# Forgetting attention: last value tiles in pieces between its first steps, results over done keys and queries

## What is computed

```python
k = kvf[..., :1024]; v = kvf[..., 1024:2048]          # kvf = rms_norm(x, kv_norm) @ w_kv, 16 heads of 64
log_f_cum = cumsum(log_sigmoid(kvf[..., 2048:] + b_forget))
q = h @ w_q
for blk in range(4):                                   # 128 queries, e = their last key
    s = q[:, :, s0:e] @ k[:, :, :e].T * 64 ** -0.5
    s = s + log_f_cum[s0:e, None] - log_f_cum[None, :e]
    p = softmax(where(mask, s, -inf))
    outs.append(p @ v[:, :, :e])
return concatenate(outs) @ w_o
```

## Time and profile before

| | us |
|---|---|
| median of 3 runs | 2179.65 (2179.22 to 2181.38) |
| profiled execution | 2178.25 |
| its span | 2176.4 |
| values of both sides up to the first scores | about 1625.5 to 1664.8 |
| attention | 1664.8 to 1743.0 |
| projection `fox_out` | from 1737.2 |

### The profile page before, as it was taken

How to read it: one execution, slowest core, us unless ns; L and a number is a source line. 1 busy time by engine, 2 the same in 40 slices (tenths; PEclk the granted TensorE clock), 3 DMA queues, 4 the chain that set the end, 5 groups by cost and what they waited for, 6 DMA issues and landing times.

```text
span 2176.4 us, 26174 instructions
## 1 busy us (share of the span) xinstructions
PE 2128.5 (98%) x10774; PEld 1699.4 (78%) x10774; DVE 1147.3 (53%) x1710; ACT 814.4 (37%) x1167; POOL 36.8 (2%) x40
## 2 busy tenths in 40 slices
PE   8999999999999999999999999999999999999998
PEld 6777678888888887787977888887787777888886
DVE  5575765442542578888836444423733746444323
ACT  4324753331232364542534222212414843332212
POOL 0120000000000000000100000000000000000000
PEclk9999999999999999999999999999999999999999
DMA  4221013222222213343121222223233022222221
GB/s 173 87 78 39 2 59 107 97 93 99 80 97 97 97 64 100 114 126 96 41 97 58 97 97 97 94 84 112 67 115 129 2 97 78 93 82 97 97 97 68
DMA packets 43112, 190.69 MB, mean 88 GB/s; under 512 B 15520, under 2 KB 16224, under 8 KB 22384
## 3 DMA queue, kind: packets, MB, share of 16 engines
q1 hardware_dynamic: 40656, 184.78, 25.3%
q10 hardware_dynamic: 2336, 4.23, 0.6%
HBM read 185.25 MB, written 3.74 MB: 87 GB/s over the span
## 4 chain that ended last, share of the span: by engine, by line
PE 51%; DVE 1%; ACT 1%; issue 0%; DVEq 0%; ACTq 0%
PE psum L441 14%; PE psum L440 14%; PE psum L442 14%; PE psum L898 1%; PE psum L881 1%; PE psum L911 1%; PE psum L451 1%; PE psum L455 1%; PE psum L452 1%; PE psum L2701 0%; PE psum L2767 0%; ACT weights_high L223 0%; DVE weights_low L250 0%; PE psum L2793 0%; PE psum L2754 0%
## 5 line engine op out<-in xcount | busy, mean ns | idle before, releaser
L250 DVE TENSOR_TENSOR weights_low<-weights_raw,weights_high 128x2048 fp32r<-128x2048 f32 (+1 forms) x161 | 365.5, 2270 | 587.9 <-ACT weights_high L223 587.8
L440 PE MATMUL psum<-split,weights_high 128*128 128x512 f32 x1448 | 574.5, 397 | 6.0 <-DVE weights_low L250 3.7
L441 PE MATMUL psum<-split,weights_high 128*128 128x512 f32 x1448 | 573.4, 396 | 0.0
L442 PE MATMUL psum<-split,weights_low 128*128 128x512 f32 x1448 | 571.8, 395 | 0.0
L223 ACT CAST weights_high<-weights_raw 128x2048 fp32r<-128x2048 f32 (+1 forms) x161 | 304.0, 1888 | 572.5 <-PE psum L442 532.9
L440 PEld LDWEIGHTS psum<-split,weights_high 128*128 128x128 f32 x1448 | 271.5, 188 | 76.7 <-issue 5.2
L442 PEld LDWEIGHTS psum<-split,weights_low 128*128 128x128 f32 x1448 | 271.5, 187 | 65.3
L441 PEld LDWEIGHTS psum<-split,weights_high 128*128 128x128 f32 x1448 | 271.6, 188 | 64.5 <-issue 0.2
L441 PE MATMUL psum<-hidden_low,weights_high 128*128 128x512 f32 x256 | 102.1, 399 | 0.0
L440 PE MATMUL psum<-hidden_high,weights_high 128*128 128x512 f32 x256 | 100.9, 394 | 0.0
L442 PE MATMUL psum<-hidden_high,weights_low 128*128 128x512 f32 x256 | 100.4, 392 | 0.0
(11 more groups left out here) (484 smaller groups left out, 3073.5 us busy)
## 6 DMA issues: line engine op xcount, KB each, us to landing
weights_raw<-in_weights SPq DMA_DIRECT2D x161, 1024.0 KB, 4.9
minus_c<-minus_c_rows ACTq DMA_DIRECT2D x16, 256.0 KB, 7.5
x_stream<-in_x SPq DMA_DIRECT2D x4, 512.0 KB, 7.2
gdn_in_grown<-gdn_rows SPq DMA_DIRECT2D x4, 512.0 KB, 4.5
chain_grown<-gdn_rows SPq DMA_DIRECT2D x4, 512.0 KB, 3.5
out<-end_results SPq DMA_DIRECT2D x8, 256.0 KB, 2.1
table<-rope_tables SPq DMA_DIRECT2D x1, 1024.0 KB, 12.4
weights_raw<-in_weights SPq DMA_DIRECT2D x1, 768.0 KB, 4.2
```

Source lines behind the costliest of these rows:

```text
L250: self.nc.vector.tensor_tensor(out=self.low_of(n)[:, 0:width], in0=self.raw[:, n % 2, 0:width], in1=self.high_of(n)[:, 0:width].bitcast(se ...
L440: nc.tensor.matmul(bank, wh, ah, start=first, stop=False)
L441: nc.tensor.matmul(bank, wh, al, start=False, stop=False)
L442: return nc.tensor.matmul(bank, wl, ah, start=False, stop=last)
```

## The change

The four tiles of side 1 are made in another order, tile by tile instead of half by half. Tiles 0 and 1 get their first half ahead of the first scores; tile 0 gets its second half behind the first scores, tile 1 its second half in turn 0 between the transposes of steps 0 and 1. Tiles 2 and 3 are made in eight pieces of 2 x 3 = 6 matmuls, one in each of turns 1 to 8, behind the first transposes of the turn and ahead of its products (`part`). Both use bank 7; ScalarE copies tiles 1, 2 and 3 out at the end of turns 0, 4 and 8 (`part_scalar`).

Since bank 7 is taken, the results of pairs 0 to 3 all go to bank 6; pair 4 uses 7, then 6, 7, 6. The products of a pair wait for the bank (`wait_results`): pair 0 for the copy of value tile 1, pairs 1 to 3 for both stored parts of the pair before, pair 4 for the last value tile, and pairs 5 to 7 as before for the pair before the last.

The tokens in `split` are now needed until turn 8, so the results go elsewhere: the high parts over the keys, the low parts over the queries of the same pair (`fox_out_split`), and `fox_out` reads them there.

The slot of the first chunk of `fox_out` is taken until turn 8 as well. Its high part is made by ScalarE at the end of turn 9 (`part_scalar`), its low part by VectorE at the end of turn 9 (`part_vector`).

```diff
@@ Attention
+            def __init__(self, ..., causal=None, beside=None):
+                self.beside = beside
             def result_bank(self, step):
-                return 6 + step // TT % 2
+                pair = step // TT
+                if self.beside is not None:
+                    return 7 if pair in (4, 6) else 6
+                return 6 + pair % 2
+            def wait_results(self, pe, pair):
+                if self.beside is None:
+                    if pair >= 2:
+                        pe.wait_ge(self.stored, pair - 1)
+                elif pair in (0, 4):
+                    self.beside.wait_results(pe, pair)
+                else:
+                    pe.wait_ge(self.stored, pair if pair < 4 else pair - 1)
@@ attend
-                if step % TT == 0 and step >= 2 * TT:
-                    pe.wait_ge(self.stored, step // TT - 1)
+                if step % TT == 0:
+                    self.wait_results(pe, step // TT)
@@ tensor
                     self.turn(pe, step)
+                    if self.beside is not None:
+                        self.beside.part(pe, step // 2)
@@ vector, after maximum(step + 3)
+                    if self.beside is not None:
+                        self.beside.part_vector(dve, step // 2)
@@ scalar, after exponent(step + 3)
+                    if self.beside is not None:
+                        self.beside.part_scalar(act, step // 2)
@@ ForgetIn
-                self.value_banks = ((4, 1, 5, 0), (4, 5, 6, 7))
-                self.last_tiles = TT // 2
+                self.value_banks = ((4, 1, 5, 0), (7, 6, 7, 7))
+                self.freed_at = 9
@@ tensor, side 1
+                pe.wait_ge(self.evicted, 2 * DT)
+                pe.wait_ge(weights.low_ready, start + self.first_value + 3)
+                for j in range(2):
+                    self.values_part(pe, 1, 0, j)
                 pe.wait_ge(self.values_read, TT)
...
+            def behind_first_scores(self, pe):
+                pe.wait_ge(weights.low_ready, self.start + self.first_value + 4)
+                self.values_part(pe, 1, 1, 0)
+            def part(self, pe, turn):
+                if turn == 0:
+                    self.values_part(pe, 1, 1, 1)
+                elif turn < self.freed_at:
+                    j, half, k = 2 + (turn - 1) // 4, (turn - 1) % 4 // 2, 2 * ((turn - 1) % 2)
+                    if half == k == 0:
+                        pe.wait_ge(self.values_read, TT + (1 if j == 2 else 3))
+                    self.values_part(pe, 1, half, j, range(k, k + 2))
+            def wait_results(self, pe, pair):
+                pe.wait_ge(self.values_read, TT + 2 if pair == 0 else 2 * TT)
+            def part_scalar(self, act, turn):
+                if turn in (0, 4, 8):
+                    self.values_out(act, 1, 1 + turn // 4)
+                if turn == self.freed_at:
+                    weights.split_high(act, Chunk(self.start + self.first_value + 4))
+            def part_vector(self, dve, turn):
+                if turn == self.freed_at:
+                    weights.split_low_vector(dve, self.start + self.first_value + 4)
@@ scalar and vector of ForgetIn: no split of chunk first_value + 4 any more
-                for n in range(self.last_query + 3, self.first_value + 5):
+                for n in range(self.last_query + 3, self.first_value + 4):
                     weights.split_low_vector(dve, start + n)
@@ places
+        fox_out_split = place("fox_out_split", 64, [P, 3, DT, T], f32r)[:, 0:3:2, :, :]
```

More of the change, by code:

```diff
@@ L849, in build_program, with __init__ @@
         class Attention:
-            def __init__(self, s, label, pairs, out_split, forget=False, prob=None, decayed=None, at=None, causal=None):
+            def __init__(self, s, label, pairs, out_split, forget=False, prob=None, decayed=None, at=None, causal=None,
+                         beside=None):
+                self.beside = beside
                 self.order, self.ahead = ((0, 2, 3, 1), 2) if forget else (range(TT), 1)
@@ L950, in wait_bank @@
                 else:
-                    pe.wait_ge(self.stored, len(self.steps) // TT - (bank == 6))
+                    last = [pair for pair in range(len(self.steps) // TT) if self.result_bank(pair * TT) == bank][-1]
+                    pe.wait_ge(self.stored, last + 1)
             def maximum(self, dve, step):
@@ L3174, in value_done @@
             def value_done(self, side, j):
+                if side == 1:
+                    return weights.tiles_before[self.start + self.first_value + 2] + (3, 4, 6, 8)[j]
                 return weights.tiles_before[self.start + self.first_value + 2 * side + 1] + j + 1
@@ L3202, in tensor, with values_part @@
                 pe.wait_ge(self.gated, 1)
[L3203 to L3213, removed]
+                for half in range(2):
+                    pe.wait_ge(weights.low_ready, start + self.first_value + half + 1)
+                    for j in range(TT):
+                        if half == 0:
+                            pe.wait_ge(self.evicted, 2 * DT - 4)
+                        self.values_part(pe, 0, half, j)
+                pe.wait_ge(self.evicted, 2 * DT)
+                pe.wait_ge(weights.low_ready, start + self.first_value + 3)
+                for j in range(2):
+                    self.values_part(pe, 1, 0, j)
                 pe.wait_ge(self.values_read, TT)
-            def values_tile(self, pe, side, half, j):
+            def values_part(self, pe, side, half, j, part=range(4)):
                 parts = weights.parts(Chunk(self.start + self.first_value + 2 * side + half), 4)
-                for k in range(4):
+                for k in part:
                     a = 4 * half + k
@@ L3221, in values_tile @@
                     last = product(psum[:, self.value_banks[side][j], :], token, [y[:, k, :] for y in parts], a == 0, a == DT - 1)
[L3222 to L3230, removed]
+                if k == 3:
+                    last.then_inc(weights.products, 1)
+            def behind_first_scores(self, pe):
[19 more added lines that the diff above has]
+                    weights.split_low_vector(dve, self.start + self.first_value + 4)
             def values_out(self, act, side, j):
@@ L3235, in values_out, with behind_first_exponents @@
                                      scale=self.entry.stat[:, 2, j:j + 1]).then_inc(self.values_read, 1)
-            def last_values_out(self, act):
-                for j in range(TT - self.last_tiles, TT):
-                    self.values_out(act, 1, j)
+            def behind_first_exponents(self, act):
+                self.values_out(act, 1, 0)
             def scalar(self, act):
@@ L3263, in scalar @@
                     act.dma_start(self.minus_c[:, h, :], self.kept[h:h + 1, :].broadcast_to([P, T])).then_inc(self.minus_c_in, 16)
[L3264 to L3269, removed]
+                weights.split_high(act, Chunk(start + self.first_value + 2))
+                for j in range(TT):
+                    self.values_out(act, 0, j)
+                weights.split_high(act, Chunk(start + self.first_value + 3))
             def vector(self, dve):
@@ L3436, in build_program @@
             fox = Attention(s, "fox", [ForgetPair(n, queries, keys, values, minus_c, minus_c_in) for n in range(FOX_HEADS // 2)],
-                            split, forget=True, prob=ring[:, 0:6, :], decayed=decayed, at=0, causal=causal)
+                            fox_out_split, forget=True, prob=ring[:, 0:6, :], decayed=decayed, at=0, causal=causal, beside=fox_in)
             last_entry = feed_forward_entry(s, 1)
-            fox_out = projection(s, "fox_out", 1, last_entry, split, fox)
+            fox_out = projection(s, "fox_out", 1, last_entry, fox_out_split, fox)
             last_ffn = feed_forward(s, 1, last_entry, fox_out.closing)
@@ L3448, in _ @@
                     fox.first_scores(pe)
-                    fox_in.last_values(pe)
-                    fox.tensor(pe, fox_in.results_free())
+                    fox_in.behind_first_scores(pe)
+                    fox.tensor(pe)
                     fox_out.tensor(pe)
@@ L3476, in _ @@
                     fox.first_exponents(act)
-                    fox_in.last_values_out(act)
+                    fox_in.behind_first_exponents(act)
                     fox.scalar(act)
```

## The result

The changed kernel takes 2186.18 us in the median of 9 runs, the kernel before 2179.11 (9 runs). Three of the nine were slow ones (2241.74, 6350.47 and 7415.16 us; among eleven more runs of the same kernel in e5 none was) and count in no comparison; the median of the other six is 2185.85, 6.7 us over the kernel before. The ratio is 1.0027, interval 1.0017 to 1.0037: 0.27% slower, or 5.9 us, with an interval of 3.7 to 8.1 us.

What follows compares the result with a forecast made beforehand. The prediction took TensorE, busy 98% of the span, as the bound, with ScalarE and VectorE close behind. Its terms -0.5 + 0.3 + 4.7 + 0.3 + 2.0 = +6.8 us on 2179.65 gave 2186.5, range 2183.0 to 2189.5.

Steps and rivals of the forecast that it cites:

- Moved TensorE work: Second-side value matmuls, 96 in both kernels: first scores start 11.3 us earlier, attention 11.3 us longer, sum 0.
- Idle time removed: Turn 0's second transposes waited 0.34 us for ScalarE's copies; twelve matmuls now stand there: -0.5 us.
- Changes of kind: Nine pieces set between TensorE's other groups cost extra spacing at each change: +0.3 us, bounds 0 and +1.8.
- ScalarE's value copies, one bank, results' place: Value copies in turns 0, 4, 8; one result bank for pairs 0 to 3; results over keys and queries: 0 each.
- The split: End of turn 9: VectorE's low half waits for ScalarE's high half, delaying normalisation and TensorE's transposes: 4.7 us idle.
- And the last piece is in turn 8: Remark in the weight-split term: the split comes at the end of turn 9, after the last piece of value matmuls.
- Behind the stall: After the idle time TensorE's products run to 1696.0, but VectorE lets it go on near 1696.3: +0.3 us.
- Clock: After the 4.7 us idle time TensorE's clock falls to 1.2 GHz for a stretch: +2.0 us, bounds 0 and +3.4.
- Rival A: The idle time at the moved weight split without a fall of the clock: +4.8 us, 2184.5; chance 0.18.
- B: Changes cost 0.2 each, copies of turns 4 and 8 show 0.5 each: +2.5 on the forecast, 2189.0; chance 0.10.
- C: Faster: pieces fill hidden ScalarE waits, eight turns give back 0.8 each, split partly covered: -5.8 us, 2174; chance 0.05.
- D: About even: idle time without the clock's fall, turns with a piece give back 0.5 each: +0.8, 2180.5; chance 0.09.

Runs made afterwards that it cites:

- e5: The changed kernel run again unchanged, as the measure for other runs on the same chip: 2185.75 us, ratio 1.0025 to the kernel before.
- e1: The changed kernel with the weight split's high half (ScalarE) at the end of turn 7, low half (VectorE) at turn 8: 2178.38 us, ratio 0.9987 to before.
- e9: The same edit to the changed kernel as e1, run again beside new runs of the kernel before: 2181.11 us, ratio 1.0002 to before.
- e4: The kernel before with one edit, all eight pairs of this attention writing results to bank 6: 2180.86 us, ratio 0.9998 to before.
- e10: The kernel before with one edit, attention results written over keys and queries and read there by fox_out: 2181.01 us, ratio 1.0002 to before.
- e3: The changed kernel with both halves of the weight split at the end of turn 7: 2187.76 us, ratio 1.0027 to before.
- e6: The changed kernel plus 17 unread matmuls (4.0 us) between turn 10's scores and step 20's transposes: 2182.71 us, ratio 1.0014 to before.
- e2: The kernel before with only the split of fox_out's first chunk moved to the end of turn 9 on both engines: 2188.39 us, ratio 1.0032 to before.
- e8: The changed kernel with the split's high half kept at turn 9, VectorE's low half moved to the end of turn 10: 2181.10 us, ratio 1.0002 to before.
- e7: The changed kernel with VectorE's low half of the split cut from 2048 to 128 columns: 2183.75 us, ratio 1.0016 to before.

## Why the prediction was right

It forecast 2186.5 us in a range of 2183.0 to 2189.5, slower with 0.83. It is 2186.18; against the forecast +6.8 stand +6.7 by the medians of the result, +5.9 by the ratio and +6.28 in the stage. Term by term:

- *Moved TensorE work, 0.* Right. The first scores came 8.95 us earlier by the clock of the trace, at 1655.86, in an execution whose attention stage had begun 2.30 later (1560.37 against 1558.07): 11.25 against the 11.3 forecast.
- *Idle time removed, -0.5.* Right: e1 and e9 show -0.54 and -0.56. Turn 0's two groups of transposes began 0.77 us apart before (1673.74 and 1674.51) and 3.07 after with 2.81 of matmuls between them, which gives 0.51, and the next transposes came 2.10 behind instead of 2.21.
- *Changes of kind, +0.3, bounds 0 and 1.8.* It is 0. From turn 2 to turn 4 one pair with two pieces took 11.20 us, which is 8.39 + 12 x 0.234. The sum 0 is also what the rule of the Trainium skill that the prediction cites (TensorE: Matmul & The Clock Gate, "Step-by-step: what each phase is for") would give, but the rows do not show free changes. In turn 3 the piece's second matmul comes 0.31 after its first and the products 0.33 after its last, against 0.23 to 0.24 in a run:

```profile
1678.34 1.09 PE L913 MATMUL psum<-const,ring 128*128 128x128 f32 x8
1679.19 0.48 PE L440 MATMUL psum<-weights_high,split 128*128 128x512 f32 x1
1679.50 0.40 PE L441 MATMUL psum<-weights_low,split 128*128 128x512 f32 x1
...
1680.43 0.40 PE L442 MATMUL psum<-weights_high,split 128*128 128x512 f32 x1
1680.76 1.09 PE L926 MATMUL psum<-fox_prob_t,fox_in_out 128*64 128x128 f32 x16
```

  What pays for these 0.18 us is the direct change that goes: the products began 1.02 after the transposes x8 in the earlier trace rows, the piece begins 0.85 after them here. The prediction had named this, and took 0.3 all the same.
- *ScalarE's value copies, one bank, results' place, 0 each.* Right but for 0.07 us. e4 shows +0.02 and e10 0.00. The next pair, with the value copy of turn 4, took 11.27: ScalarE's copy out of bank 7 ran from 1689.71 to 1690.40, and the piece of turn 5, which writes that bank again, began at 1690.46, 0.93 behind its transposes instead of 0.85. The term had looked at what waits behind the copy on ScalarE, and not at the piece that needs the bank.
- *The split, +4.7.* The mechanism is right in every link. The idle time was 4.46 us; by starts, the x16 group and the delayed x2 group are 3.39 us apart in the earlier trace rows and 7.91 here (1713.02 to 1720.93), so 4.5 late. I was 0.2 over because I added up lengths, where a record's end overlaps the start of the next one: VectorE's next instruction began 2.21 after the low half's start and not 2.29, and ScalarE's high half began 0.09 after the last exponent's second row (1716.17 and 1716.26) and not 0.20. The idle time ended at 1720.93, in an execution 2.30 late, against the forecast of near 1719.
- *"And the last piece is in turn 8."* The term sets this beside the stall, and as a reason it would be wrong. e3 has a piece in the next turn and the same 4.46: the piece stands behind the transposes that the chain ends in. What makes the cost is the series of both halves in one turn.
- *Behind the stall, +0.3.* Not seen. The products and transposes ran at half clock, which covered VectorE; and in e6, at full clock, the second transposes began at 1720.60, right behind the products.
- *Clock, +2.0, bounds 0 and 3.4.* With e1's -0.54 and the 4.5 of the wait taken off, the stage leaves 2.3 us in the changed kernel, 1.3 in e5, and 2.1 in e3; in e2, which keeps turn 0's idle time, the wait alone taken off leaves 2.1 as well. 2.0 lies among them. Rival A, the stall without the clock, was not seen in any of the five traces with an idle time of 2.46 us or more ahead of the delayed transposes; its price of +4.8 can be checked against e6, +4.08 in the stage: it is 0.7 too high, from the three small terms with 0.3, 0.2 and 0.3.
- *Rivals B, C and D.* The turns with pieces are the sum of their parts but for the 0.07 us, so nothing was given back and next to nothing was added.
- *The stages behind.* The prediction called itself wrong if one of them changed its length. From the end of the attention to the end of the span they are 0.58 us shorter in this trace, inside the 1.9 us by which this distance scatters among the traces, so no change is shown.

The three small misses (0.3, 0.2, 0.3) all went one way, and +6.28 in the stage against +6.8 is their sum with the clock's spread. That the time itself came within 0.3 us of the forecast is partly luck: the three misses were made up for by what lies outside the stage, and the difference is known only to some 2 us either way.

## What to carry to other kernels

When a step is moved into a loop whose bound engine never waits, look at who stands queued behind it, and not at the engines' shares: a producer on one engine and a consumer on another, put in the same turn, cost about their sum, and the same two a turn apart cost what each exceeds its own slack. Here that is 4.46 us for halves of 1.89 and 2.29, and a fall of the clock, against 1.1 us (e8) or nothing (e1). Work moved between other groups of a full TensorE queue cost its own length here and no more, and won nothing except the idle time that it landed in.

## What the runs showed of the hardware

An idle time of TensorE of only 2.46 us inside dense work was followed by a stretch at 1.2 GHz (e7), which the sum had left open. And the same idle time does not always do it: the one of 3.44 us in the earlier trace rows left the clock alone, while in the changed kernel's execution the same one, now 3.43, had a low stretch that began within it. Those rows of the changed kernel are:

```profile
880.73 1.94 PE L2315 MATMUL psum<-gdn_qkv,sum_selector 128*32 128x512 f32 x8 [3.43 <-ACT gdn_qkv L2446]
...
879.70:886.00 6.30, 5.27 (x20) 2.00 (x21) 6.16 (x7) 2.21 (x5) 0.00 (x0) 0.50 0.29 88
```

The kernel did not change there, and e5, the same kernel as the changed one, again kept its full clock at this place behind 3.44 us. So the stretches of low clock vary between executions of the same work, and this may be what moves the times of one kernel by some us (2178.17 to 2184.48 us for the kernel before beside e5). The stage was the steadier measure here: -0.54 and -0.56 us in e1 and e9, where the ratios were 0.9987 and 1.0002. What decides on each fall was not tried. A fall in the attention cost 1.3 to 2.3 us, about half of TensorE's busy time in the low stretch (2.90 us in e5, 3.40 in e7, 5.07 in the changed kernel).
